# A decoder stack on one core: first layer with another order of loads, splits, norm sum and group products

## Chip, core and metric

The kernel runs on one core of one Trainium2 chip. The metric is the device time of one execution in microseconds (us); lower is better. The core has five engines, each with an instruction queue of its own that runs in order: TensorE (PE, its weight load shown as PEld), VectorE (DVE), ScalarE (ACT), GpSimd (POOL) and SyncE (SP, which here only starts DMA transfers). They wait for one another by semaphores.

## What is computed

A stack of layers on x of 256 tokens by 1024 features, all in float32. The change touches the first layer only:

```python
def diff_pool_layer(x, ...):
    proj = rms_norm(x, norm_g) @ w_in                 # 1024 -> 2048: q, k, v, u of 512 each
    q, k = rms_norm(q per head, q_g), rms_norm(k per head, k_g)
    lam = exp(sum(lp[0]*lp[1])) - exp(sum(lp[2]*lp[3])) + lam_init
    a_out = diff_attention(q, k, v, lam, lam_init, sub_g)   # 4 heads, softmax 0 minus lam * softmax 1
    b_out = pool_mixer(u, w_group, pool_scale)        # 4 groups: window mean minus token, @ w_group, * scale
    return x + concat(a_out, b_out) @ w_out
```

Behind it come a gated FFN with a short convolution, a sliding-window attention layer, two more FFNs, a layer of convolution and forgetting attention, another FFN and a norm (seven phases in all: L0, F0, L1, F1, F2, MIX, F3).

## The kernel before

**Data.** The activations X lie features-first (8 tiles of 128 features by 256 tokens). All weights come in one stream of chunks of 128x2048 float32 (1 MB each): chunk i goes into raw buffer i mod 3, ACT copies it into a rounded high part `whi` (`high(i)`, line 971), DVE subtracts to get the low part `wlo` (`low(i)`, line 1473). The activations are split alike: `Ghi` on ACT is X times the norm's gain, `Glo` on DVE is the rest. Each product is three matmuls (`three`, line 300: high by high, high by low, low by high). SP sends chunk i once `low(i-3)` is done (line 288). The norm's factor is not needed by the matmuls: it multiplies their result, so the projection starts before the sum of squares is known.

**Start (`first`, lines 1086 and 1577).** SP sends X and chunk 0 in four pieces each, in turns, then the ones matrix, chunk 1 in halves, chunk 2, and three tables for later (bias_a, wgroup, invcnt). ACT sends the first gain (`par[:, 0:8]`), the rest of `par`, and the rest of `cst`. Then ACT makes, for each of the four pieces, two tiles of Ghi and then a quarter of whi; DVE follows with two tiles of Glo and a quarter of wlo. After chunk 1 the squares of X are made on ACT; POOL adds the first two, DVE adds the last two, POOL adds both sums (line 2165 on). DVE then makes the small gain products and the sum for lam (lines 1594 to 1606), ACT loads its table for Ln and Exp and takes the exponential.

**Projection (PE's `l0`, lines 598 to 632).** Output blocks of 256 columns, one chunk each; `half(b, i, h)` is one half of chunk i's eight k tiles for both 128-column blocks, 24 matmuls. Chunk 0 is done in two halves; within a half all four k tiles of the first block come before the second block. The ones matmul for the norm (`norm_sum`) stands between the two halves of chunk 1. After it ACT makes the factor (`norm_log`, line 992, which loads the table again) and DVE evacuates the first blocks (`take`). From there heads follow: squares, `blocks`, `q_factor` (ACT), `scale` (DVE), `score` (PE), `bias_in` (DVE), `exps` (ACT), `combine` (DVE), `turn` (PE transpose), `value` (PE).

**Order.** There is no planner: each engine's order is written out by hand (PE 598 to 655, ACT 1133 to 1178, DVE 1659 to 1697, POOL 2165 on). An instruction that waits holds everything behind it on its engine.

**End of the layer.** Four attention values (`value`, evacuated by ACT's `take`), four group products (`mix_groups`, split by `group` on ACT and DVE), four head norms (`norm_out`, `out`), and four chunks of the output projection (`rows`), each needing two tiles of Mhi and Mlo.

Of the kernel before, what the change touches and what calls it, by code (L numbers as in the profile page):

```python
# [5 lines left out]
ALU = mybir.AluOpType  # L6
# [4 lines left out]
P = 128  # L11
S = 256
# [11 lines left out]
for _n, _w in (("ab_norm", 8), ("c_norm", 8), ("f_norm0", 8), ("f_norm1", 8), ("ffn1_norm", 8), ("mix_norm", 8),  # L24
               ("ffn2_norm", 8), ("a_q", 1), ("a_k", 1), ("a_sub", 1), ("b_scale", 4), ("c_q", 1), ("c_k", 1),
               ("conv0", 3 * 44), ("conv1", 3 * 44), ("convb0", 44), ("convb1", 44), ("conv_w", 31 * 4),
               ("conv_b", 4), ("ln_g", 4), ("ln_b", 4), ("onc", 4), ("ona", 4), ("forget_b", 1), ("sinks", 32),
               ("lam", 256)):
    PAR[_n] = (_at, _w)
    _at += _w  # L30
# [95 lines left out]
def program(nc, x, wst, par_d, cst_d, bias_a_d, bias_c_d, invcnt_d, wgroup_d, fin_d, out):  # L126
    ctx = ExitStack()
    with ctx:
# [18 lines left out]
        X = sb("X", [P, DT, S])  # L147
# [68 lines left out]
        s_gain, s_par, s_cst, s_ones = sem("s_gain"), sem("s_par"), sem("s_cst"), sem("s_ones")  # L216
# [50 lines left out]
        def _(sp):  # L267
            for j in range(4):
                ws = slice(512 * j, 512 * j + 512)
                sp.dma_start(X[:, 2 * j:2 * j + 2, :], two(x[:, ws])).then_inc(s_xin[j], 16)  # L270
                sp.dma_start(raw[:, 0, ws], wst[0][:, ws]).then_inc(s_w0[j], 16)
# [5 lines left out]
            sp.dma_start(bias[:, 0:4 * S], bias_a_d).then_inc(s_ba, 16)  # L277
            sp.dma_start(wgroup, two(wgroup_d)).then_inc(s_wg, 16)
            sp.dma_start(invcnt, invcnt_d.rearrange("p (a b) -> p a b", a=4)).then_inc(s_ic, 16)
            for i in range(3, NCH):  # L280
# [8 lines left out]
                sp.dma_start(raw[:, i % NR, w], wst[i][:, w]).then_inc(s_raw[i % NR], 16)  # L289
            for n, (t, h) in enumerate(((0, 0), (0, 1), (1, 0), (1, 1))):  # L290
# [5 lines left out]
        def _(pe):  # L296
# [11 lines left out]
            def half(b, i, h, ph=None):  # L308
# [5 lines left out]
                for n in range(2):  # L314
                    for k in range(4 * h, 4 * h + 4):
                        if n == 0 and ph is not None:
                            pe.wait_ge(s_glo, 8 * ph + k + 1)
                        if n == 0 and i < 2 and k % 2 == 0:
                            pe.wait_ge(s_lo, k // 2 + 1 if i == 0 else 5 + k // 4)
# [3 lines left out]
                if h == 1:  # L323
                    last.then_inc(s_used, 1)

# [27 lines left out]
            def norm_sum(ph, by_log):  # L353
                pe.wait_ge(s_sum, SUMS[ph])
                if ph == L0:
                    pe.wait_ge(s_ones, 16)
                else:
                    pe.wait_ge(s_x, 4 * ph)
# [187 lines left out]
            def l0():  # L546
# [87 lines left out]
                value(1)  # L634
# [3 lines left out]
                turn(2)  # L638
                pe.wait_ge(s_vt, 2)
# [322 lines left out]
        def _(act):  # L962
# [29 lines left out]
            def norm_log(ph, n):  # L992
                table()
# [92 lines left out]
            def first():  # L1086
                act.dma_start(par[:, 0:8], par_d[:, 0:8]).then_inc(s_gain, 16)
                act.dma_start(par[:, 8:NPAR], par_d[:, 8:NPAR]).then_inc(s_par, 16)
                act.dma_start(cst[:, 128:NCST], cst_d[:, 128:NCST]).then_inc(s_cst, 16)
                act.wait_ge(s_gain, 16)  # L1090
                for j in range(4):
                    ws = slice(512 * j, 512 * j + 512)
                    act.wait_ge(s_xin[j], 16)
                    for n in (2 * j, 2 * j + 1):
                        act.activation(Ghi[:, n, :], X[:, n, :], ACT.Copy, scale=col("ab_norm", n)).then_inc(s_ghi, 1)
                    act.wait_ge(s_w0[j], 16)
                    copy(whi[:, 0, ws], raw[:, 0, ws]).then_inc(s_hi, 1)
                for j in range(2):
# [3 lines left out]
                for j, o in enumerate((sq[:, 0, :], sq[:, 1, :], QR[:, 0, :], QR[:, 1, :])):  # L1102
                    act.activation(two(o), X[:, 2 * j:2 * j + 2, :], ACT.Square).then_inc(s_sq, 1)
                act.wait_ge(s_par, 16)
                act.wait_ge(s_lsum, 1)
                table()
                act.activation(lamt[:, 2:4], lamt[:, 0:2], ACT.Exp).then_inc(s_lexp, 1)

            def l0():
# [23 lines left out]
                high(2)  # L1133
# [327 lines left out]
        def _(dve):  # L1461
# [115 lines left out]
            def first():  # L1577
                dve.memset(eps[:, :], EPS).then_inc(s_eps, 1)
                dve.wait_ge(s_gain, 16)
                for j in range(4):  # L1580
                    ws = slice(512 * j, 512 * j + 512)
                    dve.wait_ge(s_xin[j], 16)
                    for n in (2 * j, 2 * j + 1):
                        dve.wait_ge(s_ghi, n + 1)
                        STT(Glo[:, n, :], X[:, n, :], col("ab_norm", n), f(Ghi[:, n, :]), ALU.mult, ALU.subtract).then_inc(s_glo, 1)
                    dve.wait_ge(s_hi, j + 1)
                    TT(wlo[:, 0, ws], raw[:, 0, ws], f(whi[:, 0, ws]), ALU.subtract).then_inc(s_lo, 1)
                for j in range(2):
# [752 lines left out]
```

## Time and profile before

| | |
|---|---|
| runs | 1067.52, 1065.29, 1066.82 us; median 1066.82 us |
| profiled execution | 1067.42 us, span 1065.6 us |
| mean granted TensorE clock | 0.994 of full |
| PE busy | 1027.7 us, 96% of the span |
| DVE, ACT, POOL busy | 732.4, 609.0, 345.7 us |
| read from memory | 181.39 MB |

The profiled execution is one run; its span is 1.8 us shorter than its own time. "Busy" counts instructions from start to end, and matmuls overlap, so a busy PE is not PE at its peak. A wait is given in square brackets behind an instruction: how long its engine idled before it, and who released it. The first layer fills about the first 100 us of the span.

### The profile page before, as it was taken

What the parts mean: (1) busy time and instruction counts of PE and PEld (TensorE: products, weight loads), DVE (VectorE), ACT (ScalarE), POOL (GpSimd) and SP (SyncE); (2) the same over time, 40 slices, a digit from 0 to 9 for tenths busy, and PEclk for the clock granted to TensorE, in tenths of its full rate; (3) what the DMA queues carried; (4) which work ended last, traced back from release to release, by engine and by line L of the source; (5) the groups of instructions that cost most, each with busy time, mean ns of one, the idle gap of its engine ahead of it and who ended that gap; (6) DMA issues with size and microseconds to landing.
All of it is one profiled execution on the core that took longest, in us unless ns stands there. A gap on an engine that the chain in (4) does not pass through costs nothing.

```text
span 1065.6 us, 17048 instructions
## 1 busy us (share of the span) xinstructions
PE 1027.7 (96%) x7078; PEld 941.7 (88%) x7078; DVE 732.4 (69%) x992; ACT 609.0 (57%) x841; POOL 345.7 (32%) x189
## 2 busy tenths in 40 slices
PE   6999999999999899999999999999999799999997
PEld 5889999998888799999888888888899598888886
DVE  5876898775548779887647766653799778666543
ACT  6765656653356657565436655543667776555631
POOL 1061264540000024545202455510148413555300
PEclk9999999999999999999999999999999899999999
DMA  8544665446432255555554655555245136555451
GB/s 320 205 147 141 255 212 185 166 151 237 159 119 80 69 189 198 205 191 164 197 193 141 242 186 181 198 197 193 102 160 167 72 120 219 190 183 197 139 177 40
DMA packets 27292, 183.53 MB, mean 172 GB/s; under 512 B 3152, under 2 KB 3280, under 8 KB 5968
## 3 DMA queue, kind: packets, MB, share of 16 engines
q1 hardware_dynamic: 26784, 181.74, 48.5%
q8 instruction: 56, 0.92, 0.3%
q10 hardware_dynamic: 432, 0.71, 0.2%
q14 instruction: 20, 0.16, 0.0%
HBM read 181.39 MB, written 1.05 MB: 171 GB/s over the span
## 4 chain that ended last, share of the span: by engine, by line
PE 85%; ACT 4%; DVE 4%; issue 3%; POOL 2%; DMA 1%; SPq 0%; DVEq 0%; POOLq 0%; ACTq 0%
PE psum L298 84%; POOL Y L2107 2%; ACT Pb L1075 1%; DVE Pb L1572 1%; DMA raw<-in_wst 1%; DVE wlo L1465 1%; ACT whi L969 1%; ACT Ob L1273 1%; DVE X L1471 1%; ACT Pb L1282 0%; DVE bias L1471 0%; DVE Pb L1468 0%; ACT PT L969 0%; PE psum L530 0%; POOL acc L2107 0%
## 5 line engine op out<-in xcount | busy, mean ns | idle before, releaser
L298 PE MATMUL psum<-G,whi 128*128 128x256 f32 (+1 forms) x2720 | 613.0, 313 | 9.7 <-DVE wlo L1465 9.7
L1465 DVE TENSOR_TENSOR wlo<-raw,whi 128x2048 fp32r<-128x2048 f32 (+1 forms) x172 | 389.3, 2275 | 205.0 <-ACT whi L969 204.9
L298 PEld LDWEIGHTS psum<-G,whi 128*128 128x128 f32 x2720 | 445.6, 190 | 44.2 <-DVE G L1471 8.4
L298 PE MATMUL psum<-G,wlo 128*128 128x256 f32 x1712 | 481.1, 281 | 0.0
L969 ACT ACTIVATE whi<-raw 128x2048 fp32r<-128x2048 f32 (+1 forms) x172 | 318.8, 1866 | 173.5 <-PE psum L298 164.4
L298 PEld LDWEIGHTS psum<-G,wlo 128*128 128x128 f32 x1712 | 324.1, 189 | 0.1
L298 PE MATMUL psum<-A,whi 128*128 128x512 f32 x528 | 183.2, 392 | 0.0
L2107 POOL TENSOR_TENSOR A<-Ab,A 128x512 fp32r<-128x512 f32 x44 | 124.9, 2839 | 139.6 <-ACT A L969 139.6
L2107 POOL TENSOR_TENSOR Ab<-Cb 128x512 f32<-128x512 f32 x44 | 117.5, 2670 | 116.1 <-ACT Cb L1010 116.1
L298 PE MATMUL psum<-A,wlo 128*128 128x256 f32 x528 | 147.3, 279 | 0.0
L298 PEld LDWEIGHTS psum<-A,whi 128*128 128x128 f32 x528 | 98.8, 187 | 22.0
L2107 POOL TENSOR_TENSOR acc<-sq 128x512 f32<-128x512 f32 x7 | 9.1, 1298 | 319.5 <-ACT sq L990 303.3
L298 PEld LDWEIGHTS psum<-A,wlo 128*128 128x128 f32 x528 | 99.6, 189 | 0.0
L1035 ACT ACTIVATE Cb<-Hb,par 128x256 f32<-128x256 f32 x88 | 47.4, 595 | 61.6 <-DVE Hb L1465 61.6
L1471 DVE SCALAR_TENSOR_TENSOR Cb<-Hb,par,Cb 128x256 f32<-128x256 f32 x176 | 78.0, 503 | 0.9
L298 PE MATMUL psum<-Mhi,whi 128*128 128x256 f32 x192 | 55.5, 289 | 1.0 <-DVE Mlo L1465 1.0
L298 PE MATMUL psum<-whi,A 128*128 128x512 f32 x176 | 54.6, 390 | 0.0
L298 PE MATMUL psum<-Mhi,wlo 128*128 128x256 f32 x192 | 54.3, 283 | 0.0
L298 PE MATMUL psum<-Mlo,whi 128*128 128x256 f32 x192 | 54.3, 283 | 0.0
L969 ACT ACTIVATE Cb<-psum 128x512 f32<-128x512 f32 x44 | 25.7, 589 | 48.5 <-PE psum L298 48.5
L2107 POOL TENSOR_TENSOR Y<-Y,Ob 128x256 f32<-128x256 f32 x41 | 41.6, 1015 | 12.2 <-ACT Ob L1273 4.7
L1465 DVE TENSOR_TENSOR Cb<-psum,Cb 128x512 f32<-128x512 f32 x44 | 29.8, 684 | 22.9 <-ACT Cb L969 22.9
(176 smaller groups left out, 1005.5 us busy)
## 6 DMA issues: line engine op xcount, KB each, us to landing
raw<-in_wst SPq DMA_DIRECT2D x165, 1024.0 KB, 4.9
bias<-in_bias_c SPq DMA_DIRECT2D x1, 2048.0 KB, 8.7
raw<-in_wst SPq DMA_DIRECT2D x3, 512.0 KB, 7.5
X<-in_x SPq DMA_DIRECT2D x4, 256.0 KB, 6.6
raw<-in_wst SPq DMA_DIRECT2D x4, 256.0 KB, 6.9
out<-bias SPq DMA_DIRECT2D x4, 256.0 KB, 2.0
bias<-in_bias_a SPq DMA_DIRECT2D x1, 512.0 KB, 11.1
bias<-in_invcnt SPq DMA_DIRECT2D x1, 512.0 KB, 12.0
```

The source lines that it names most:

```text
L298: return pe.matmul(o, a, b, start=start, stop=stop, skip_group_check=True)
L969: return act.activation(o, i, ACT.Copy)
L1035: act.activation(Cb[:, p % 2, e, :], Hb[:, p % 2, e, 2:S + 2], ACT.Identity, scale=col(f"conv{conv}", 2 * 44 + ch), bias=col(f"convb{conv} ...
L1075: last = act.activation(Pb[:, e, m, c0:c1], Pb[:, e, m, c0:c1], ACT.Exp, bias=st[:, e, 4 + k_:5 + k_], accum_out=st[:, e, 8 + k_:9 + k_])
L1273: act.activation(PR[:, q % 4, :], UP[:, i, j:j + S], ACT.Copy, scale=col("conv_w", 4 * j + i)).then_inc(s_prod, 1)
L1465: return dve.tensor_tensor(o, a, b, op)
L1471: return dve.scalar_tensor_tensor(o, a, s, b, op0, op1)
L1572: dve.tensor_tensor_reduce(Pb[:, e, m, c0:c1], bank[banks[m]][:, c0:c1], bias_of(m)[:, S - nk:S], 1.0, init_of(m), ALU.add, ALU.max, st[:, ...
L2107: return pool.tensor_tensor(o, a, b, op)
```

## The change

The layout of the first layer is changed; what is computed stays the same.

- **Loads.** The first norm's gain moves out of `par` and stands in front of x in one array, so that it comes with the first piece of X. SP sends only the X pieces; chunk 0's four pieces are sent by ACT's queue, at the same time. `par` (now one transfer) goes behind chunk 3, bias_a behind chunk 4, wgroup and invcnt behind chunk 5. The rest of `cst` goes behind chunk 2.
- **Splits.** Per piece ACT makes one Ghi tile, the quarter of whi, the second Ghi tile; DVE likewise.
- **PE.** Chunk 0 is multiplied piece by piece (`first_chunk`): two k tiles for both column blocks, then the next piece. `norm_sum` stands behind chunk 1.
- **Norm sum.** First square ahead of chunk 1's split, the second between its halves. POOL adds squares 0, 1 and 2; DVE adds the fourth.
- **Table.** ACT loads Ln/Exp's table once, behind its four DMA starts; the two later loads are gone.
- **Small products.** The gains and lam's sum go into DVE's `l0` behind `low(2)`, lam's end behind `take(1)`. One `q_factor` moves ahead of `high(4)`, one `scale` ahead of `low(4)`.
- **End of the layer.** Groups stand between values: `mix_groups(0)` and `turn(2)` before `value(1)`, `mix_groups(3)` behind the first `rows`, `group` likewise on ACT.

```diff
+        gain_x = sb("gain_x", [P, DT + DT * S])
+        X = gain_x[:, DT:].rearrange("p (a b) -> p a b", a=DT)
@@ block.sync
             for j in range(4):
-                ws = slice(512 * j, 512 * j + 512)
-                sp.dma_start(X[:, 2 * j:2 * j + 2, :], two(x[:, ws])).then_inc(s_xin[j], 16)
-                sp.dma_start(raw[:, 0, ws], wst[0][:, ws]).then_inc(s_w0[j], 16)
+                ws = slice(512 * j + (DT if j else 0), 512 * j + DT + 512)
+                sp.dma_start(gain_x[:, ws], x[:, ws]).then_inc(s_xin[j], 16)
...
-            sp.dma_start(bias[:, 0:4 * S], bias_a_d).then_inc(s_ba, 16)
-            sp.dma_start(wgroup, two(wgroup_d)).then_inc(s_wg, 16)
-            sp.dma_start(invcnt, ...).then_inc(s_ic, 16)
+            sp.dma_start(cst[:, 128:NCST], cst_d[:, 128:NCST]).then_inc(s_cst, 16)
             for i in range(3, NCH):
...
+                if i == 3:
+                    sp.dma_start(par[:, :], par_d).then_inc(s_par, 16)
+                if i == 4:
+                    sp.dma_start(bias[:, 0:4 * S], bias_a_d).then_inc(s_ba, 16)
+                if i == 5:
+                    sp.dma_start(wgroup, ...); sp.dma_start(invcnt, ...)
@@ block.tensor
+            def first_chunk(b):
+                h3, l3 = weights(0, DT)
+                for j in range(4):
+                    for n in range(2):
+                        ws = slice(n * P, n * P + P)
+                        for k in (2 * j, 2 * j + 1):
+                            if n == 0:
+                                pe.wait_ge(s_glo, k + 1)
+                                pe.wait_ge(s_lo, j + 1)
+                            last = three(...)
...
-                half(5, 0, 0, L0)
-                half(5, 0, 1, L0)
+                first_chunk(5)
                 half(4, 1, 0)
+                half(4, 1, 1)
                 norm_sum(L0, True)
+                half(6, 2, 0)
                 pe.wait_ge(s_cst, 16)
-                half(4, 1, 1)
-                half(6, 2, 0)
                 blocks(0, 7)
...
                 value(0)
-                value(1)
                 pe.wait_ge(s_wg, 16)
                 pe.wait_ge(s_vt, 1)
                 mix_groups(0, 5)
                 turn(2)
+                value(1)
...
                 pe.wait_ge(s_m0, L0_M[4])
                 mix_groups(1, 5)
-                pe.wait_ge(s_m0, L0_M[6])
-                mix_groups(3, 4)
                 value(3)
                 norm_out(1)
                 rows(0, 2)
+                pe.wait_ge(s_m0, L0_M[6])
+                mix_groups(3, 4)
@@ block.scalar, first
-                act.dma_start(par[:, 0:8], ...); act.dma_start(par[:, 8:NPAR], ...); act.dma_start(cst[:, 128:NCST], ...)
-                act.wait_ge(s_gain, 16)
+                for j in range(4):
+                    act.dma_start(raw[:, 0, ws], wst[0][:, ws]).then_inc(s_w0[j], 16)
+                table()
                 for j in range(4):
                     act.wait_ge(s_xin[j], 16)
-                    for n in (2 * j, 2 * j + 1):
-                        act.activation(Ghi[:, n, :], X[:, n, :], ACT.Copy, scale=col("ab_norm", n))
+                    act.activation(Ghi[:, 2 * j, :], X[:, 2 * j, :], ACT.Copy, scale=gain_x[:, 2 * j:2 * j + 1])
                     act.wait_ge(s_w0[j], 16)
                     copy(whi[:, 0, ws], raw[:, 0, ws]).then_inc(s_hi, 1)
+                    act.activation(Ghi[:, 2 * j + 1, :], ...)
+                square(0, sq[:, 0, :])
                 for j in range(2):
                     copy(whi[:, 1, ws], raw[:, 1, ws]).then_inc(s_hi, 1)
+                    if j == 0:
+                        square(1, sq[:, 1, :])
-                (four squares, wait for par and lsum, table(), Exp for lam)
+                square(2, QR[:, 0, :]); square(3, QR[:, 1, :]); high(2)
@@ block.scalar, l0
                 norm_log(L0, 0)                       # without its table()
                 q_square(0)
                 q_square(1)
+                act.wait_ge(s_lsum, 1)
+                act.activation(lamt[:, 2:4], lamt[:, 0:2], ACT.Exp).then_inc(s_lexp, 1)
                 high(3)
+                q_factor(0, 7)
                 high(4)
-                q_factor(0, 7)
...
                 take(0)
+                group(0, 5)
+                turned(2)
                 take(1)
-                turned(2)
-                group(0, 5)
+                group(2, 4)
                 take(2)
-                group(2, 4)
                 turned(3)
                 out(0)
+                group(1, 5)
                 take(3)
-                group(1, 5)
@@ block.vector, first
-                TT(QR[:, 0, :], QR[:, 0, :], QR[:, 1, :], ALU.add).then_inc(s_sqa, 1)
-                (gains, lam's sum, lam)
+                dve.wait_ge(s_sum, 2)
+                TT(acc[:, :], acc[:, :], QR[:, 1, :], ALU.add).then_inc(s_sqa, 1)
@@ block.vector, l0
                 low(2)
+                gains()
                 take(0)
                 take(1)
+                lam()
                 low(3)
+                scale(0)
                 low(4)
-                scale(0)
@@ block.gpsimd, l0
-                pool.wait_ge(s_sqa, 1)
+                pool.wait_ge(s_sq, 3)
```

## Rows read from the trace of the kernel before

**Rows 1.** Page, part 4: chain that ended last, by engine
```profile
PE 85%; ACT 4%; DVE 4%; issue 3%; POOL 2%; DMA 1%; SPq 0%; DVEq 0%; POOLq 0%; ACTq 0%
```

**Rows 2.** Timeline of the start: start us, us, engine, line, what [idle before <-releaser]
```profile
4.55 0.47 SPq L271 DMA_DIRECT2D raw<-in_wst  x1
4.81 1.28 ACT L1095 ACT_TABLE_LOAD   x1 [4.81 <-DMA X<-in_x]
...
7.56 0.69 DVE L1465 TENSOR_TENSOR wlo<-raw,whi 128x512 fp32r<-128x512 f32 x1
...
8.40 0.77 PE L298 MATMUL psum<-G,whi 128*128 128x256 f32 x2 [8.40 <-DVE wlo L1465]
...
10.46 0.61 ACT L969 ACTIVATE whi<-raw 128x512 fp32r<-128x512 f32 x1
10.47 0.77 PE L298 MATMUL psum<-G,whi 128*128 128x256 f32 x2 [0.45 <-DVE wlo L1465]
...
11.81 0.62 ACT L969 ACTIVATE whi<-raw 128x512 fp32r<-128x512 f32 x1
...
20.04 1.13 PE L298 MATMUL psum<-acc,cst 128*128 128x256 f32 x4 [0.55 <-POOL acc L2107]
...
24.93 0.50 PE L298 MATMUL psum<-G,whi 128*128 128x256 f32 x2 [0.89 <-DVE wlo L1465]
```

**Rows 3.** DMA issues, one window each: out<-in, queue, count, KB, us to landing
```profile
raw<-in_wst SPq DMA_DIRECT2D x1, 256.0 KB, 7.1
par<-in_par ACTq DMA_DIRECT2D x1, 421.0 KB, 5.8
...
raw<-in_wst SPq DMA_DIRECT2D x1, 1024.0 KB, 9.4
```

**Rows 4.** Stretches: A:B us, length, (PE busy (x count),) PEclk, DMA share, GB/s
```profile
5.00:12.00 7.00, 1.00 1.04 393
...
8.40:12.30 3.90, 3.45 (x14) 1.00 1.05 402
13.00:19.00 6.00, 6.00 (x53) 1.00 1.03 414
```

**Rows 5.** Timeline of ACT and DVE around the norm's factor
```profile
22.57 1.28 ACT L966 ACT_TABLE_LOAD   x1
22.58 2.29 DVE L1465 TENSOR_TENSOR wlo<-raw,whi 128x2048 fp32r<-128x2048 f32 x1 [1.46 <-ACT whi L969]
...
24.89 1.29 DVE L1465 TENSOR_TENSOR QR<-psum,R 128x512 f32<-128x512 f32 x2
```

**Rows 6.** Timeline of DVE, PE and POOL, middle of the layer
```profile
45.45 0.68 DVE L1465 TENSOR_TENSOR QR<-psum,R 128x512 f32<-128x512 f32 x1
...
47.69 0.40 PE L298 MATMUL psum<-G,whi 128*128 128x256 f32 x2
...
53.21 2.61 POOL L2107 TENSOR_TENSOR T<-UP 128x271 f32<-128x271 f32 x1 [33.13 <-DVE UP L1465]
...
57.43 0.63 POOL L2107 TENSOR_TENSOR T<-UP 128x271 f32<-128x271 f32 x1
...
57.61 0.74 DVE L1471 SCALAR_TENSOR_TENSOR QK<-QR,gsc,sq 128x256 f32<-128x256 f32 x1 [0.35 <-ACT sq L1068]
...
59.37 0.18 DVE L1629 RECIPROCAL st<-st 128x4 f32<-128x4 f32 x1 [0.25 <-ACT Pb L1075]
...
62.76 2.83 DVE L1465 TENSOR_TENSOR wlo<-raw,whi 128x2048 fp32r<-128x2048 f32 x1
```

**Rows 7.** Timeline of the layer's end
```profile
68.77 0.84 ACT L1082 ACTIVATE Vt<-psum,rcol 128x256 f32<-128x256 f32 x2
...
70.31 0.91 PE L298 MATMUL psum<-PT,Vt 128*128 128x128 f32 x6 [0.90 <-ACT Y L1119]
...
75.14 0.70 PE L298 MATMUL psum<-UP,bias 128*128 128x256 f32 x2 [0.87 <-DVE Mlo L1471]
...
76.59 0.47 PE L298 MATMUL psum<-Mhi,whi 128*128 128x256 f32 x1
```

More of the change, by code:

```diff
@@ L23 @@
 _at = 0
[L24 removed]
+for _n, _w in (("c_norm", 8), ("f_norm0", 8), ("f_norm1", 8), ("ffn1_norm", 8), ("mix_norm", 8),
                ("ffn2_norm", 8), ("a_q", 1), ("a_k", 1), ("a_sub", 1), ("b_scale", 4), ("c_q", 1), ("c_k", 1),
@@ L289, in _ @@
                 sp.dma_start(raw[:, i % NR, w], wst[i][:, w]).then_inc(s_raw[i % NR], 16)
+                if i == 3:
[3 more added lines that the diff above has]
+                if i == 5:
+                    sp.dma_start(wgroup, two(wgroup_d)).then_inc(s_wg, 16)
+                    sp.dma_start(invcnt, invcnt_d.rearrange("p (a b) -> p a b", a=4)).then_inc(s_ic, 16)
             for n, (t, h) in enumerate(((0, 0), (0, 1), (1, 0), (1, 1))):
@@ L324, in half @@
                     last.then_inc(s_used, 1)
+            def first_chunk(b):
[7 more added lines that the diff above has]
+                                pe.wait_ge(s_lo, j + 1)
+                            last = three(bank[b][:, n * S:n * S + S], h3[:, k, ws], l3[:, k, ws], Ghi[:, k, :], Glo[:, k, :],
+                                         k == 0 and n == 0, k == DT - 1)
+                last.then_inc(s_used, 1)
             def wide(b, i, h, ph=None):
@@ L992, in norm_log @@
             def norm_log(ph, n):
-                table()
+                if ph != L0:
+                    table()
                 act.wait_ge(s_nrm, ph + 1)
@@ L1086, in first @@
             def first():
-                act.dma_start(par[:, 0:8], par_d[:, 0:8]).then_inc(s_gain, 16)
-                act.dma_start(par[:, 8:NPAR], par_d[:, 8:NPAR]).then_inc(s_par, 16)
-                act.dma_start(cst[:, 128:NCST], cst_d[:, 128:NCST]).then_inc(s_cst, 16)
-                act.wait_ge(s_gain, 16)
+                for j in range(4):
+                    ws = slice(512 * j, 512 * j + 512)
+                    act.dma_start(raw[:, 0, ws], wst[0][:, ws]).then_inc(s_w0[j], 16)
+                table()
                 for j in range(4):
@@ L1093, in first, with square @@
                     act.wait_ge(s_xin[j], 16)
-                    for n in (2 * j, 2 * j + 1):
-                        act.activation(Ghi[:, n, :], X[:, n, :], ACT.Copy, scale=col("ab_norm", n)).then_inc(s_ghi, 1)
+                    act.activation(Ghi[:, 2 * j, :], X[:, 2 * j, :], ACT.Copy, scale=gain_x[:, 2 * j:2 * j + 1]).then_inc(s_ghi, 1)
                     act.wait_ge(s_w0[j], 16)
                     copy(whi[:, 0, ws], raw[:, 0, ws]).then_inc(s_hi, 1)
+                    act.activation(Ghi[:, 2 * j + 1, :], X[:, 2 * j + 1, :], ACT.Copy, scale=gain_x[:, 2 * j + 1:2 * j + 2]).then_inc(s_ghi, 1)
+                def square(j, o):
+                    act.activation(two(o), X[:, 2 * j:2 * j + 2, :], ACT.Square).then_inc(s_sq, 1)
+                square(0, sq[:, 0, :])
                 for j in range(2):
@@ L1101, in first @@
                     copy(whi[:, 1, ws], raw[:, 1, ws]).then_inc(s_hi, 1)
[L1102 to L1107, printed above, removed]
+                    if j == 0:
+                        square(1, sq[:, 1, :])
+                square(2, QR[:, 0, :])
+                square(3, QR[:, 1, :])
+                high(2)
             def l0():
@@ L1641, in combine, with gains, lam @@
                     last.then_inc(s_prob, 1)
+                def gains():
+                    dve.wait_ge(s_par, 16)
+                    TS1(gsc[:, 0:1], col("a_q"), 0.125, ALU.mult)
+                    TS1(gsc[:, 1:2], col("c_q"), 0.125, ALU.mult)
+                    TS1(gsc[:, 2:3], col("a_sub"), 0.8, ALU.mult).then_inc(s_gsc, 1)
+                    l4 = par[:, PAR["lam"][0]:PAR["lam"][0] + 256].rearrange("p (a b c) -> p a b c", a=2, b=2)
+                    lt = T[:, 0, 0:128].rearrange("p (a c) -> p a c", a=2)
+                    TT(lt, l4[:, :, 0, :], l4[:, :, 1, :], ALU.mult).then_inc(*own.up())
+                    dve.wait_ge(s_vec, own.n)
+                    dve.tensor_reduce(lamt[:, 0:2], lt, mybir.AxisListType.X, ALU.add).then_inc(s_lsum, 1)
+                def lam():
+                    dve.wait_ge(s_lexp, 1)
+                    TT(lamt[:, 4:5], lamt[:, 2:3], lamt[:, 3:4], ALU.subtract).then_inc(*own.up())
+                    dve.wait_ge(s_vec, own.n)
+                    TS1(lamt[:, 6:7], lamt[:, 4:5], 0.8 - 0.6, ALU.add).then_inc(s_lam, 1)
                 def take_u(c):
@@ L2293, in cols @@
         return a.reshape(-1, P).T
-    put("ab_norm", cols(v["ab_norm"][0]))
     put("c_norm", cols(v["c_norm"][0]))
```

35 lines of the change are left out of this document (11 added, 24 removed).

## The prediction

> **What bounds the kernel now.** I read four views. The chain that ended last says that PE carries the time [rows 1]: a microsecond counts where PE stands still or starts late. So the timeline of the first layer comes next, for PE's waits. Up to the first output rows there are six: 8.40 us before the first matmul, 0.45 at 10.47, 0.55 at 20.04, 0.89 at 24.93 [rows 2], and two of about 0.9 at the layer's end, told below. Between 24.93 and those two it never waits. The third view, DMA issues with their landings, says what the early waits hang on. Chunk 0's last piece was sent at 4.55 and landed 7.1 us later, at 11.65 [rows 2, 3]; ACT took it at 11.81 [rows 2]. From 5 to 12 us the transfers run at 393 GB/s with the DMA engines' share at 1.04 [rows 4], so the first pieces are paced by bytes, not by starts. The fourth, the other engines' timeline, shows who releases PE later.
>
> **The start.** (1) The table load at 4.81 lasts 1.28 us and begins when X's first piece is there [rows 2]. In the changed kernel it runs right behind ACT's four DMA starts (about 0.45 us each, the length of SP's start [rows 2], so until 2.6) and ends near 3.9, before any data: hidden. Its cover is the 4.8 us of the first landing. (2) `par`, 421 KB [rows 3], and `cst` (530 columns of 128 rows by 4 bytes, 265 KB) no longer run among the first pieces. Of X and chunk 0, 2048 KB, the last then lands 686 KB earlier, at 393 GB/s 1.8 us: 11.65 becomes 9.9. A piece pair of 512 KB takes 1.3 us, so the pairs are in at about 5.5 to 6.0, 7.3, 8.6 and 9.9. That chunk 0 goes over the other queue saves starts, which were not the bound; I cost it at nothing. (3) X's first piece at 4.9; chunk 0's first I take at 5.5, since two 256 KB pieces now share the rate. Then whi 0.61, wlo 0.69 with hand-overs: PE starts at 7.0. Bounds: 6.4 if the weights land with X, 8.1 if they land at 6.6. The two Ghi tiles round the copy cost nothing: they fill the wait for the weights. Before it was 8.40: **-1.4**.
>
> **Chunks 0 and 1.** From 8.40 to 24.93 PE took 16.53 us. Its three waits sum to 1.89 [rows 2]; a matmul's record lasts 0.16 us beyond the start of the next, so by starts each wait is 0.16 longer: 2.4 in all. Without them 14.1. PE's slow beginning stays in: 14 matmuls in 3.45 busy us against 53 in 6.00 later [rows 4], a surcharge of some 1.8 us, though the granted clock stands at 1.00 in both stretches. I carry it over unchanged. ACT's pace is one piece per 1.35 us (10.46 to 11.81 [rows 2]), so pieces are ready on DVE at about 7.3, 9.3, 10.9 and 12.4. PE, four triples a piece, wants them from 7.0, 9.6, 11.5 and 13.0: no wait, chunk 0 ends at 14.4. For chunk 1 DVE is ready at 14.35, just in time. `norm_sum`, now behind both halves, waits for nothing if the sum is there by 20.2.
>
> **DVE against POOL.** POOL's first two sums now run while DVE splits chunk 1. The rows show that such pairs take turns: POOL's 0.63 us addition took 2.61 beside a split that had started just before, and a split of 2.29 took 2.83 when POOL was first [rows 5, 6]. By that, POOL's first sum waits until 14.35 and ends at 15.6, the second half of chunk 1 runs to 16.8, POOL's second sum to 18.1, DVE's own to 18.75, `low(2)` to 21.05. PE wants `low(2)` at 21.0. So `half(6,2,0)` starts at **21.1** where it was 24.93, **-3.8**. The Trainium skill ("SBUF — State Buffer", Who interferes with whom) has the rule: the pair of ports is an exclusive lock, and a DVE instruction with two SBUF inputs blocks a reading GpSimd one. The trace agrees by the 2.61. Without the rule `low(2)` would be there at 20.0 and PE at 21.0, so it takes 0.1 us and all the slack.
>
> **Norm factor and heads.** The second table load (1.28 at 22.57 [rows 5]) is gone from ahead of Ln; Ln and Exp follow the sum at 21.1, and `take(0)` starts at 22.05 instead of 24.89 [rows 5]: 2.85 earlier. The gains (six small DVE instructions, with hand-overs 0.9 us together; such a one lasts about 0.18 [rows 6]) fit between `low(2)` and this. lam's exponential costs ACT 0.2 us ahead of `high(3)`. So ACT and DVE run 2.6 us early, PE 3.8: PE gains 1.2 on them. Its closest claim on them in the middle is `take(3)`, which ended at 46.1 for matmuls at 47.7 [rows 6]: 1.5 us of slack, so it still does not wait. DVE loses its waits of 0.35 and 0.25 [rows 6], because PE is ahead: it reaches the last scores, and ACT the last exponentials, 3.25 early. `take_v(1)` starts at 65.5 where it was 68.77 [rows 7].
>
> **The order at the end.** `value(1)` needs `take(0)` and starts 1.5 us after `take_v(1)` as before. But `mix_groups(0)` and `turn(2)`, 0.5 and 0.3 us of PE by the length of the same instructions' neighbours (0.70 for two passes with their tail, 0.91 for six small matmuls [rows 7]), now lie under its wait of 0.90, and the 0.87 us wait at 75.14 [rows 7] falls away since `mix_groups(3)` comes behind 5.8 us of `rows`. I take 0.6 and 0.85: **-1.4**. Behind this the order is PE's own and its tiles come in time: tile 5 at 73.4 for 74.3, tile 1 at 79.1 for 81. Everything later moves as a block.
>
> **DMAs on SP's queue.** SP's waits for chunks 3 to 5 come earlier with the splits. The tables put behind them are wanted late: `cst` at 24.1 (lands near 16), bias_a at 33.4, invcnt at 50. Only `par` is close; it is a rival below.
>
> **Sum.** -3.25 (last exponentials) -1.4 = -4.65 us. The profiled execution took 1067.42, so 1062.8; it stands 0.6 above the median of 1066.82, from which the sum gives 1062.2. I say 1062.6.
>
> **Rivals.**
> (a) *Pieces land later.* If the two queues don't share evenly and X and chunk 1 run ahead of chunk 0, or w0's first piece needs until 6.6 and each wait reappears, PE gains 1.5 to 2.5 at the start instead of 3.8. With the end's 1.4 and what slack takes up: 1064 to 1065. For: the engines are full from 5 us. Against: fewer bytes in front. The Trainium skill ("DMA: Bandwidth & Descriptors", Issuing engines are not separate DMA queues) says that transfers of all queues interleave on the same 16 engines; the share of 1.04 agrees. That speaks for sharing, and against a gain from the second queue. Chance 0.13.
> (b) *The lock goes the other way.* If POOL's second sum gets its turn before the half split, or another operation is held too, `low(2)` comes at 22.3, PE waits 1.2, and the gains and `take(0)` come 1 us later: 1063.8. Chance 0.12.
> (c) *The table is loaded again* before the first copy, 1.28 us at X's landing as now: PE starts at 8.1 and the lost microsecond stays: 1063.8. Against: copies and squares behind the load at 22.57 ran without another. Chance 0.04.
> (d) *Slower: the gains hold DVE.* `gains()` waits for `par`, and behind it on DVE stand `take(0)` and all heads. `par` is now sent behind chunk 3, at about 12.1. By bytes: 3823 KB behind chunk 0's last piece, 10 us: 19.8, wanted at 21.1. Upper bound: chunk 3's 9.4 us [rows 3] and 1.1 for `par`'s bytes: 22.6, costing 1.5. Each later microsecond costs one; the gain is used up when `par` lands at 21.1 + 4.65 = 25.8, and at 28 the time is 1069. Nothing in the rows reaches that. With any mishap of that size, chance 0.04.
>
> **How the numbers follow.** Forecast 0.67, (a) 0.13, (b) 0.12, (c) 0.04, (d) 0.04. A measurement of this kernel tells about 0.2%, 2.1 us, from no change: faster is below 1064.7. The forecast, (b), (c) and half of (a) lie below, less a little for sizes that are off together: faster 0.85, same 0.11, slower 0.04. The range's lower end has PE start at 6.4, no lock, and DVE's waits in the middle shrinking too: 6 us off, 1060.9. The upper end takes in (b), (c) and most of (a): 1064.9.
>
> **What would show it.** PE's first matmul at 7.0; no wait of PE over 0.2 us until past 60; `low(2)` ending near 21; one table load in the layer's start, before 4 us; `take(0)` at 22; the wait before `value(1)` still there but short, none before `mix_groups(3)`; the first output rows at about 71.5. The prediction is wrong if ACT still waits for chunk 0's pieces, if DVE's first gain starts after 21.5, or if a new wait of PE stands ahead of `turn(3)`, where its probabilities come only just in time.

## The result, and the profile after

The changed kernel takes 1056.39 us (median of 4 runs, 1054.56 to 1058.33); the kernel before takes 1066.28 us beside it (4 runs). The ratio is 0.9905, with a 95% interval from 0.9893 to 0.9918: **faster by about 10 us**. The forecast was 1062.6, with 1060.9 to 1064.9 as its range. So the sign was right, but the time lies 4.5 us below the range, and more than half of the gain was not foreseen. The profiled spans are 1065.6 us before and 1056.5 after.

Part 4 of the page after, the chain that ended last, by engine:

```profile
PE 83%; DVE 7%; ACT 6%; issue 2%; POOL 1%; DMA 0%; DVEq 0%; ACTq 0%; POOLq 0%
```

PE still carries the time, as in [rows 1]. The timeline of the first layer after, with the columns of [rows 2]:

```profile
2.62 1.28 ACT L986 ACT_TABLE_LOAD   x1 [2.62 <-issue]
...
4.86 0.61 ACT L989 ACTIVATE whi<-raw 128x512 fp32r<-128x512 f32 x1
...
6.35 0.76 PE L304 MATMUL psum<-G,whi 128*128 128x256 f32 x2 [6.35 <-DVE wlo L1490]
...
13.34 1.81 POOL L2142 TENSOR_TENSOR acc<-sq 128x512 f32<-128x512 f32 x1 [12.90 <-ACT sq L1120]
14.24 1.99 DVE L1490 TENSOR_TENSOR wlo<-raw,whi 128x1024 fp32r<-128x1024 f32 x1 [0.24 <-ACT whi L989]
15.30 2.08 POOL L2142 TENSOR_TENSOR acc<-acc,QR 128x512 f32<-128x512 f32 x1
...
18.03 2.28 DVE L1490 TENSOR_TENSOR wlo<-raw,whi 128x2048 fp32r<-128x2048 f32 x1
...
19.77 1.02 PE L304 MATMUL psum<-acc,cst 128*128 128x256 f32 x4
20.23 0.27 DVE L1493 TENSOR_SCALAR gsc<-par 128x1 f32<-128x1 f32 x3
20.44 0.59 PE L304 MATMUL psum<-G,whi 128*128 128x256 f32 x2
21.92 1.29 DVE L1490 TENSOR_TENSOR QR<-psum,R 128x512 f32<-128x512 f32 x2 [0.91 <-ACT R L1018]
...
64.36 0.81 ACT L1103 ACTIVATE Vt<-psum,rcol 128x256 f32<-128x256 f32 x2
...
65.86 0.91 PE L304 MATMUL psum<-PT,Vt 128*128 128x128 f32 x6 [0.53 <-ACT Y L1143]
...
69.65 0.94 PE L304 MATMUL psum<-PT,Vt 128*128 128x128 f32 x6 [0.37 <-ACT PT L989]
70.67 0.47 PE L304 MATMUL psum<-Mhi,whi 128*128 128x256 f32 x1
```

What to see here: one table load, under the first transfers; PE's first matmul at 6.35, where it was 8.40 [rows 2]; `half(6,2,0)` at 20.44, where it was 24.93 with a wait of 0.89; `take(0)` at 21.92 for 24.89 [rows 5]; the first output rows at 70.67 for 76.59 [rows 7]. The landings of the three transfers in question, one row each (KB, us from issue to landing):

```profile
gain_x<-in_x SPq DMA_DIRECT2D x1, 260.0 KB, 3.7
raw<-in_wst ACTq DMA_DIRECT2D x1, 256.0 KB, 3.9
par<-in_par SPq DMA_DIRECT2D x1, 421.0 KB, 7.3
```

**Where the time went outside the layer.** PE executes the same list of matmuls outside the first layer, so the n-th matmul of one trace can be set against the n-th of the other. After minus before, in us from the span's start (worked out from the traces' records):

```
n-th matmul          80    440    680   1700   2100   5400   6000    7000
time before        21.5   68.8  101.1  223.7  290.5  776.1  863.8  1041.4
after - before    -3.58  -4.83  -5.49  -8.78  -7.77 -10.52  -8.90   -9.10
```

By the layer's output rows (n=680) the gain is 5.5 us. Another 3.3 comes in the first FFN's up projection (to n=1700), 1 is lost in its down projection, and the second FFN does the same again. The 256-column products of L1 and MIX give 0.4 and 1.0 more, so that the gain stands at 11.2 at n=5600; some 2 of it are lost between 790 and 840 us. In none of these FFN stretches does PE wait: the matmuls themselves follow one another faster or slower. The view of stretches shows it: 150 to 200 us lies in F0's up projection, 235 to 275 in its down projection, 600 to 650 in F2. The columns are PE's busy time, its count, the granted clock, the DMA share and GB/s. First the kernel before:

```profile
150.00:200.00 50.00, 50.00 (x419) 1.00 0.51 178
235.00:275.00 40.00, 40.00 (x233) 1.00 0.59 208
600.00:650.00 50.00, 50.00 (x290) 1.00 0.57 193
```

and after:

```profile
150.00:200.00 50.00, 50.00 (x431) 1.00 0.58 206
235.00:275.00 40.00, 40.00 (x228) 1.00 0.60 212
600.00:650.00 50.00, 50.00 (x291) 1.00 0.55 192
```

PE is busy for the whole stretch and at a clock of 1.00 in all six, but in the first it does 431 matmuls instead of 419, in the second 228 instead of 233. Taken from start to start, the mean step of F0's and F1's up projection is 120.0 ns before and 116.7 after; of their down projection (a matmul of 512 columns and one of 256 in turns; the mean of both, per matmul) 173.3 before and 176.7 after; of F2 (the same turns) 173.3 in both. Below, such a triple stands as "steps up / down / F2". These matmuls run in fp32r, the rounded float32 of `whi`, `wlo` and G, each behind a weight load of its own.

The loss around 800 us is the granted clock. In every trace it falls there for some microseconds to half of full speed, and for how long differs between executions of one kernel. The kernel before, the same again (e4), the changed kernel, and the same again (e3):

```profile
785.00:850.00 65.00, 56.53 (x421) 0.92 0.33 114
785.00:850.00 65.00, 56.56 (x421) 0.92 0.34 114
785.00:850.00 65.00, 57.23 (x396) 0.87 0.28 98
785.00:850.00 65.00, 57.59 (x415) 0.89 0.28 98
```

By the records, the clock stands at half in this stretch for 10.2, 10.2, 17.1 and 13.7 us. The two traces of the changed kernel agree within about 0.3 us up to n=5800; then the second is ahead, by 11.07 at n=7000 where the first has 9.10. So up to 2 us of the table's last columns belong to that one execution (1058.33 us, the slowest of its four) and not to the change.

### The profile page after: what moved, and what is told of

Same layout as the page of the kernel before. It is cut to its first block, busy times and chain, and to the rows that moved or that the text cites. A ratio compares the mean times of both kernels' runs of the same rounds, so it can differ in the third digit from the quotient of the medians.

```text
span 1056.5 us, 17049 instructions
## 1 busy us (share of the span) xinstructions
PE 1023.8 (97%) x7078; PEld 938.3 (89%) x7078; DVE 732.9 (69%) x992; ACT 605.4 (57%) x839; POOL 349.5 (33%) x189
## 4 chain that ended last, share of the span: by engine, by line
PE 83%; DVE 7%; ACT 6%; issue 2%; POOL 1%; DMA 0%; DVEq 0%; ACTq 0%; POOLq 0%
PE psum L304 83%; DVE wlo L1490 2%; ACT whi L989 1%; ACT Pb L1096 1%; DVE gain_x L1496 1%; DVE Pb L1597 1%; POOL Y L2142 1%; ACT Ob L1298 1%; DVE Pb L1493 0%; ACT Pb L1307 0%; DMA gain_x<-in_x 0%; DVE G L1496 0%; DVE bias L1496 0%; ACT PT L989 0%; DVE QK L1496 0%
## 5 line engine op out<-in xcount | busy, mean ns | idle before, releaser
L304 PE MATMUL psum<-G,whi 128*128 128x256 f32 (+1 forms) x2720 | 603.9, 310 | 6.4 <-DVE wlo L1490 6.3
L304 PE MATMUL psum<-A,whi 128*128 128x512 f32 x528 | 185.5, 396 | 0.0
L2142 POOL TENSOR_TENSOR A<-Ab,A 128x512 fp32r<-128x512 f32 x44 | 130.8, 2973 | 135.4 <-ACT A L989 135.4
L2142 POOL TENSOR_TENSOR Ab<-Cb 128x512 f32<-128x512 f32 x44 | 114.1, 2592 | 110.9 <-ACT Cb L1031 110.9
L2142 POOL TENSOR_TENSOR Y<-Y,Ob 128x256 f32<-128x256 f32 x41 | 41.6, 1015 | 13.7 <-ACT Ob L1298 6.1
```

The source lines that it names most:

```text
L304: return pe.matmul(o, a, b, start=start, stop=stop, skip_group_check=True)
L2142: return pool.tensor_tensor(o, a, b, op)
```

## The experiments

The diff has one side effect that the first runs follow up. `gain_x` holds 8 floats in front of X, so X and the two tiles behind it in SBUF (G2 for the high and low FFN activations, and `cst`, whose first 128 columns are the ones matrix of every norm sum) each lie 32 bytes further back in every partition; `par` is 32 bytes shorter, so that all behind it lies as before. Theory A: this shift sets the pace of the matmuls. Rival B: how the program starts, or its instruction stream, sets it. Rival C: it varies from run to run.

**e1: the shift alone, in the kernel before.**

```diff
+        gain = sb("gain", [P, DT])          # in front of X
...
-                act.dma_start(par[:, 0:8], par_d[:, 0:8]).then_inc(s_gain, 16)
+                act.dma_start(gain[:, :], par_d[:, 0:8]).then_inc(s_gain, 16)
```

> The kernel before, with one edit: the first norm's gain has a tile of its own (32 bytes a partition) in front of X, so that X, G2 and cst lie 32 bytes further on, exactly where the changed kernel has them; every order and every transfer stays. The two traces differ in the start-to-start step of the matmuls of the first up projection (120.0 ns before, 116.7 ns after) and of the first down projection (173.3 and 176.7 ns). Theory A, the step hangs on where G2 lies: 116.7 ns here too, and the time falls by the 3.6 us that the trace shows behind the first layer, to about 1062.7, with the first layer as before (first output rows at 76.6 us). Rival B, the step hangs on how the program starts or on its instruction stream: 120.0 ns and 1066.3 us as before. Rival C, it changes from run to run: either of the two, also between the repeated runs.

Measured: 1061.85 us against 1067.12, ratio 0.9948 (0.9933 to 0.9963). Up to n=680 it runs as before (-0.09), at n=1700 it is 3.38 ahead, and at n=5600, before the clock falls, 6.08. Its three stretches:

```profile
150.00:200.00 50.00, 50.00 (x431) 1.00 0.53 181
235.00:275.00 40.00, 40.00 (x228) 1.00 0.59 211
600.00:650.00 50.00, 50.00 (x291) 1.00 0.54 188
```

The counts are those of the changed kernel. **The shift alone gives 5.3 us**; none of this depends on the first layer's order. The start and the order of all instructions are those of the kernel before, so rival B falls; e2 shows it from the other side.

**e2: the changed kernel without the shift** (the gain in a tile of its own behind `cst`, with one small transfer more behind X's first piece).

```diff
-        gain_x = sb("gain_x", [P, DT + DT * S])
-        X = gain_x[:, DT:].rearrange("p (a b) -> p a b", a=DT)
+        X = sb("X", [P, DT, S])
...
+        gain_x = sb("gain_x", [P, DT])
```

> The changed kernel with the reverse edit: the gain has a tile of its own behind cst, so that X, G2 and cst lie where the kernel before has them, and one small transfer more runs behind X's first piece. Theory A (place of G2): the matmul step of the first up projection goes back to 120.0 ns and the time rises by about 3.6 us to 1060; the first layer keeps its order and its output rows start within 0.5 us of the changed kernel's 70.7. Rival B (start or instruction stream): 116.7 ns and 1056.4 us, plus up to 0.4 for the extra transfer.

Measured: 1062.26, ratio 0.9954 (0.9938 to 0.9971), so 4.9 us gained, and the stretches count as before. The expectation had the step right and the time 2.3 us too low, because it took the shift's worth from the first trace as 3.6:

```profile
150.00:200.00 50.00, 50.00 (x420) 1.00 0.56 192
235.00:275.00 40.00, 40.00 (x233) 1.00 0.64 226
600.00:650.00 50.00, 50.00 (x290) 1.00 0.54 189
```

This is the kernel that the forecast costed, with its 4.65. The two halves, 5.3 and 4.9, make 10.2 of the 10.8 that the changed kernel gains against the same runs (e3).

**e3 and e4: both kernels again**, unchanged, measured beside e1 and e2.

> The changed kernel, unchanged, once more. Theories A and B: the same steps as in its first profile, 116.7 and 176.7 ns, and 1056.4 us within 0.2%. Rival C (from run to run): another step in this profile, and runs several microseconds apart.

> The kernel before, unchanged, once more, for a second profile of it. Theories A and B: steps of 120.0 and 173.3 ns as in its first profile and 1066.3 us within 0.2%. Rival C: other steps.

Measured: 1056.32 (ratio 0.9896, 0.9882 to 0.9911) and 1066.98 (0.9999, 0.9989 to 1.0008), each with the steps that it had. Rival C falls for the steps; for the granted clock around 800 us it holds, as shown above.

**e5 to e8: which tile's place matters?** e5 puts the 32 bytes between G2 and `cst`, e6 between X and G2; e7 moves X, G2 and `cst` by 64 (and by 32 some small tiles behind them); e8 moves A2, the FFN's hidden activations, by 32 and nothing else. The edit in each is e1's, or:

```diff
+            sb("ahead_of_A2", [P, 8], F32, reg)      # e8
```

> The kernel before with the gain's 32-byte tile between G2 and cst: X and G2 stay, only cst moves by 32 bytes. Theory A1 (it is G2, the moving operand of all projections, whose place sets the step): matmul step of the first up projection 120.0 ns, time 1067 us as before. Rival A2 (the tile's 32 bytes anywhere, or cst's place): 116.7 ns and about 1062.

> The kernel before with the gain's tile between X and G2: X stays, G2 and cst move by 32 bytes. Theory A1: 116.7 ns in the up projections, 176.7 ns in the first two down projections, time 1062 us as with X moved too. Rival A3 (X's place, which only ACT and DVE read): 120.0 ns and 1067 us.

> The kernel before with 64 bytes ahead of X instead of 32, so that G2 lies 64 bytes off its old place; A2 stays where it is (two small tiles are merged to make room). Is the fast step bound to an odd multiple of 32 bytes? Theory A1a (the rows of 64 bytes count): 120.0 ns and 1067 us again. Rival A1b (any place other than the old one, a multiple of 128 bytes, is good): 116.7 ns and about 1062.

> The kernel before with 32 bytes ahead of A2, the moving operand of the down projections; G2 stays. Theory A1 (the place of the moving operand sets the step of the products that read it): up projections stay at 120.0 ns, the first two down projections change from 173.3 ns. Rival A4 (the down step hangs on G2's place too, by the history of the stream): 173.3 ns and 1067 us. No sign is forecast for the time: by up to 3.3 ns in each of some 350 matmuls of two phases, 2 us either way.

| run | moved | us | ratio (95%) | steps up / down / F2, ns |
|---|---|---|---|---|
| before | nothing | 1067.25 | 1 | 120.0 / 173.3 / 173.3 |
| e5 | `cst` 32 | 1074.21 | 1.0070 (1.0053 to 1.0088) | 120.0 / 176.7 / 176.7 |
| e6 | G2, `cst` 32 | 1061.70 | 0.9950 (0.9936 to 0.9965) | 116.7 / 176.7 / 173.3 |
| e7 | G2, `cst` 64 | 1068.45 | 1.0019 (1.0009 to 1.0028) | 117.8 / 176.7 / 175.5 |
| e8 | A2 32 | 1068.15 | 1.0010 (1.0000 to 1.0020) | 120.0 / 173.3 / 173.3 |

e6 equals e1: X's place does not matter. e7 met neither of its theories (its 175.5 is 176.7 in F2's up and 173.3 in its down projection). e5 kept the up step that its theory A1 expected, but neither time came: `cst` alone makes the kernel 7 us slower, in stretches whose long run of matmuls never reads `cst`:

```profile
150.00:200.00 50.00, 50.00 (x419) 1.00 0.52 177
235.00:275.00 40.00, 40.00 (x228) 1.00 0.59 201
600.00:650.00 50.00, 50.00 (x285) 1.00 0.57 199
```

The up projection keeps its 419; the down projection falls to 228 and F2 from 290 to 285. In F3, too, the mean step of the up projection rises from 173.3 to 176.7. So there are at least two things, one that hangs on G2 and one on something in `cst`; and they act together, since with both moved (e6) F2 and F3 keep 173.3.

e8 seems to do nothing, but the three steps leave out F3's last product, which reads A2 in 512 columns. There the mean step is 226.7 ns in the kernel before and 233.3 in e8, 1.7 us in all. The kernel before, then e8:

```profile
1000.00:1055.00 55.00, 55.00 (x252) 1.00 0.29 101
1000.00:1055.00 55.00, 55.00 (x246) 1.00 0.28 96
```

So A2's place counts as well, in that product.

**e11: `cst` moved as in e5, but the ones matrix left in its old place.** Theory S1: what matters in `cst` is the norm sum's read of the ones.

```diff
+        ones = sb("ones", [P, 128])[:, :]
+        gain = sb("gain", [P, DT])
-        cst = sb("cst", [P, NCST])
+        cst = sb("cst", [P, NCST - 128])
```

> The kernel that was 7 us slower (only cst moved by 32 bytes) with one edit: the ones matrix, the part of cst that the norm sums read, goes back to its old place in a tile of its own; identity, block matrix and mask stay moved. Theory S1 (the norm sum's matmul, reading ones 32 bytes off, leaves the slow step behind in all that follows): 173.3 ns down, time back at 1067. Rival S2 (another reader of cst, or the place of something else): 176.7 ns and 1074.

Measured: 1066.94, ratio 1.0001 (0.9992 to 1.0010), steps as before:

```profile
150.00:200.00 50.00, 50.00 (x419) 1.00 0.50 177
235.00:275.00 40.00, 40.00 (x233) 1.00 0.59 210
600.00:650.00 50.00, 50.00 (x290) 1.00 0.56 194
```

The whole 7 us of e5 hangs on the ones matrix, which is read by a few matmuls before each FFN (and by some in L0, L1 and MIX) and by none within the stretches. A short read sets the pace of hundreds of later matmuls. By the records the pattern of single steps changes directly behind F0's norm sum: in e11 the up projection goes 117, 118, 121, 120, 124 ns over and over, in e5 it goes 120 each time. The mean is the same, so the up projection's time does not show it; 960 matmuls later the down projection has 173.3 in e11 and 176.7 in e5.

**e9 and e13: the changed kernel with `cst` (and all behind it) 128 and 512 bytes further**, to see whether the fast up projection can be had with the fast down projection. e9 does it with one unused tile of 24 floats; e13 with three small tiles that lay elsewhere, and 8 floats.

```diff
+        sb("ahead_of_cst", [P, 24])        # e9
```

> The changed kernel with 96 bytes ahead of cst and 32 behind par: G2 keeps the place that gave 116.7 ns in the up projections, while cst and everything behind it lie 128 bytes on from the places of the kernel before, a whole multiple of 64. So far every kernel with cst off by 32 or 64 bytes had 176.7 ns in the first two down projections, every one with cst in its old place 173.3. Theory S (the place of cst, which the norm sum reads just ahead of them, leaves the slow step behind): 116.7 ns up and 173.3 ns down, about 2.3 us less than the changed kernel, 1054. Rival R (the down step hangs on G2's place or on the gain's tile): 176.7 ns and 1056.4.

> The changed kernel with cst, and all behind it, 512 bytes on from the places of the kernel before (three small tiles fill the room), G2 where the changed kernel has it. With 128 bytes the down step was 175.6 ns instead of 176.7 and the up step 117.0 to 117.8. Theory S (the place of ones alone sets the down step, with a period of 512 bytes or less): 116.7 ns up, 173.3 ns down, some 2 us less than the changed kernel. Rival (the down step hangs on G2 and ones together, and G2's 32 bytes keep it slow): 175 to 177 ns and 1056 to 1058 us.

Measured: e9 1057.62, ratio 0.9918 (0.9899 to 0.9937), steps 116.7 to 117.8 / 175.6 / 174.1; e13 1055.57, ratio 0.9902 (0.9886 to 0.9919), steps 116.7 / 176.7 / 173.3. Neither is told apart from the changed kernel (0.9905). The simple form of the theory, in which the down projection hangs on the ones' place alone, fell.

**e14 to e16: does an additional matmul do it, with nothing moved?** In the kernel before, each FFN's norm sum gets one more matmul, into columns that nothing reads. In e14 its weights lie 32 bytes off the ones; e15 is the control with the ones themselves; e16 is e14 with the additional one first.

```diff
-                    mm(bank[at(ph, 3)][:, 0:S], ones, acc[:, 0:S], True, True).then_inc(s_nrm, 1)
+                    mm(bank[at(ph, 3)][:, 0:S], ones, acc[:, 0:S], True, True)
+                    mm(bank[at(ph, 3)][:, S:512], cst[:, 8:136], acc[:, 0:S], True, True).then_inc(s_nrm, 1)
```

> The kernel before, no tile moved, with one matmul more behind the norm sum of each of the four FFNs: the same acc, but as weights cst from column 8 on, 32 bytes off the ones matrix, into a part of the bank that nobody reads (so nothing of the result changes). Theory S (a weight read 32 bytes off leaves the slower step behind): 176.7 ns in the down projections of F0 and F1 and in F2, as in the kernel whose cst had moved, and 1067 + 7 + 4 x 0.45 = about 1075 us. Rival T (such a read costs its own time only): 173.3 ns and 1069.

> Control to the kernel before it: the same extra matmul, with the ones matrix itself, in its old place, as weights. Theory S and rival T alike: 173.3 ns and about 1069 us. If the step changes here too, it is not the 32 bytes but any further matmul that shifts it.

> The extra matmul 32 bytes off ahead of the norm sum's own, which then reads ones in its old place last. Theory S1 (the last read counts): 173.3 ns down, about 1069 us. Rival S2 (an off-place read is kept and not undone by one in place): 176.7 ns and about 1075.

Measured: 1074.47 (1.0080, 1.0065 to 1.0095), 1073.88 (1.0081, 1.0066 to 1.0096) and 1076.90 (1.0104, 1.0089 to 1.0119), all three with steps 120.0 / 176.7 / 176.7. The control's stretches:

```profile
150.00:200.00 50.00, 50.00 (x419) 1.00 0.51 181
235.00:275.00 40.00, 40.00 (x228) 1.00 0.57 197
600.00:650.00 50.00, 50.00 (x285) 1.00 0.57 200
```

They count as e5's, though no tile was moved, and the up projection has e5's pattern of 120 each time. The control itself is what taught something here: in F0, F1 and F2 the 32 bytes are not needed, either additional matmul does it. F3 is different: its up projection stays at 173.3 in e14 and e15 and goes to 176.7 in e16 (as in e5), which is worth 2.1 of the 2 to 3 us by which e16 is slower than they are. e14 and e16 have the same matmuls there and differ in the order of two.

The additional matmuls take 1.7 us of their own (0.43 each; the group of norm sums takes 7.4 us in place of 5.7), and the slower steps in F0, F1 and F2 add 5.6 in the traces. e14's trace, whose clock stands at half as long as that of the kernel before (10.2 us), ends 7.1 us later. The medians say 8.4 (e15) because the runs of the kernel before beside these had a median of 1065.47, where it was 1067 elsewhere; all seven of them had a mean granted clock of 0.996 or more.

So **the pace of a long run of matmuls depends on which matmuls ran before it**, and the places of their operands act through that or beside it. Which property is carried over was not found. One rival stands untested: an additional matmul also moves every later instruction of PE's stream by one. It can't explain e5 against e11, or e14 against e16 in F3, where the counts are the same.

**e10 and e12: the layer's end and its start apart.** e10 is the kernel before with the new order of the end alone; e12 is e2 with the old one, so the start alone.

```diff
                 value(0)
-                value(1)
                 ...
                 mix_groups(0, 5)
                 turn(2)
+                value(1)
```

> The kernel before with the new order of the layer's end alone (groups between values, the last group product behind the first output rows, on PE and ACT). By the prediction's term: 1.4 us less than before, 1065.6, the wait of 0.87 us ahead of mix_groups(3) gone and the output rows 1.9 us earlier in the trace, 0.45 of it only moved. Rival (the order pays only when PE runs ahead of ACT): no difference, because PE waits the same time for take(0) and turned(3).

> The changed kernel with G2 and cst in their old places and with the old order of the layer's end: loads, splits, norm sum, table and small products alone. With G2 and cst in place the whole change gave 4.9 us. By the prediction's terms 3.25 of it come from here: 1064.0. Rival (the start gives all and the end nothing): 1062.3.

Measured: e12 1063.51, ratio 0.9971 (0.9960 to 0.9982), so 3.5 us, for an expected 1064.0. e10 1066.33, ratio 0.9997 (0.9988 to 1.0006), for an expected 1065.6: not resolved by its times as they stand. Its trace has the rows earlier, though:

```profile
74.08 0.94 PE L298 MATMUL psum<-PT,Vt 128*128 128x128 f32 x6 [0.37 <-ACT PT L969]
...
75.10 0.47 PE L298 MATMUL psum<-Mhi,whi 128*128 128x256 f32 x1
```

75.10 for 76.59, and -1.06 us at n=680. The two waits of about 0.9 are gone and a new one of 0.37, on ACT's evacuation for `turn(3)`, stands in their place. e12 shows both old waits again:

```profile
66.72 0.91 PE L305 MATMUL psum<-PT,Vt 128*128 128x128 f32 x6 [0.90 <-ACT Y L1144]
...
71.56 0.70 PE L305 MATMUL psum<-UP,bias 128*128 128x256 f32 x2 [0.87 <-DVE Mlo L1497]
...
73.01 0.47 PE L305 MATMUL psum<-Mhi,whi 128*128 128x256 f32 x1
```

Between e2 and e12 the medians differ by 1.25 us and n=680 by 1.17 (-4.75 and -3.58). The end's order is worth 1.1 to 1.2 in the traces. The medians of all runs show 0.7 of it (1066.33 for 1067.02); among the runs with a mean granted clock of 0.994 or 0.993 alone, e10's eight have a median of 1066.57 and the eleven of the kernel before 1067.64, which is 1.1.

## Why the prediction was right in part

**The start: right, a little short.** Forecast 7.0, measured 6.35. The table load is hidden, as said (2.62 to 3.90). The step that was too careful is the landing of chunk 0's first piece: I took 5.5, and it came at about 4.6, together with X's (3.9 and 3.7 us from their issues). ACT's queue sent it while SP's sent X, so the second queue, which I costed at nothing, is the likely giver of these 0.6 us; it was not tried alone. In e2, with one small transfer more, PE starts at 6.70. What was measured lies at the lower bound of 6.4.

**Chunks 0 and 1: right.** PE has no wait between 6.35 and 65.86. `half(6,2,0)` stands at 20.44 for a forecast of 21.1: the 0.66 of the start, carried through.

**DVE against POOL: the mechanism right, rival (b) not seen.** POOL's two sums take 1.81 and 2.08 us, and the half split between them 1.99 where the first half took 1.23. In the kernel before, the first sum, which ran almost alone, took 1.29:

```profile
16.62 1.29 POOL L2107 TENSOR_TENSOR acc<-sq 128x512 f32<-128x512 f32 x1 [16.18 <-ACT sq L1103]
```

The ends lie as turns would have them: the first half split at 14.01 (12.78 and 1.23), POOL's first sum at 15.15, the second half split at 16.23, POOL's second sum at 17.38. The Trainium skill ("SBUF — State Buffer", Who interferes with whom) has this as an exclusive lock of the shared port pair; the trace agrees. This is the order that I laid out, with each end 0.3 to 0.7 us earlier than forecast, as PE's start was: `low(2)` ends at 20.3 for 21.05. It costs PE nothing.

**Norm factor and heads: right, 1.1 too little at their end.** `take(0)` at 21.92 for 22.05, `take_v(1)` at 64.36 for 65.5. `take_v(1)` is 4.41 earlier, as much as PE (4.49 at `half(6,2,0)`): between `take(0)`, 2.97 earlier, and there ACT and DVE catch up 1.4 us where I had allowed 0.4. Which waits gave it was not broken down.

**Rivals (a), (c) and (d)** did not occur: pieces on time, no second load, `par` in at 19.3 (its 7.3 us behind an issue at 12.0; I had 19.8) and the gains at 20.23, directly behind `low(2)`.

**The end: right, too large.** Forecast -1.4, measured -1.1 to -1.2. The 0.87 wait fell away as said; what I named in the last sentence as a possible fault, a new wait ahead of `turn(3)`, is there with 0.37, and in the changed kernel 0.53 of the wait before `value(1)` stays.

**The sum for the layer**: forecast -4.65; measured -4.75 at n=680 in e2 (and -4.9 in its time; in between, its profiled execution lost 1.4 while the clock stood at half near 372 us, and got 2.0 back near 830, where it did so for 3.4 us less), where PE starts at 6.70 and `take_v(1)` at 65.08; and -5.5 in the changed kernel (4.41 at `take_v(1)` and 1.1 for the end).

**The step that failed** is "Everything later moves as a block." The prediction has no term for what the new tile `gain_x` does to the places of the tiles behind it; it put this at nothing, without a reason. The shift was worth -5.3 us by itself (e1), all of it far behind the changed layer: about -3.3 in each up projection of F0 and F1, +1 in each of their down projections, and -0.7 and -1.0 in L1 and MIX. That is 6.1 up to n=5600; in e1's trace 0.8 of it is given back at the lower granted clock around 830 us. No row of the trace of before could have given this size; but no row excluded it either, and nothing in the range stood for it. The range's lower end of 1060.9 allowed 6 us, the measured gain was 10.

**What stays open.** Shown are: the place of G2 changes the up projection's step, the place of the ones matrix the down projection's, F2's and F3's, the place of A2 that of F3's last product, and one additional matmul in each norm sum does in F0, F1 and F2 what the moved ones matrix did. Not shown is the rule: e7's in-between steps, F3 in e14 to e16, and e9 and e13, where the step of the down projection is 175.6 and 176.7 with `cst` 128 and 512 bytes on, do not fit one period or one overlap. Whether the change makes the granted clock stand at half for longer around 800 us is open too: the two traces of the changed kernel have 17.1 and 13.7 us of it, but e13, with the same first layer, has 10.2 like the kernel before.

## What to carry to other kernels

Where PE is the bound and never waits, compare the step from one matmul's start to the next in stretches that the change does not touch, before giving a difference to the part that was edited; a tile put in front of others is an edit to all of them. To cost a new layout of loads, add it once with the tiles left where they were (as e2 does): that run tells the schedule's worth from the layout's. The order of the start could be forecast here from landings and waits to within a microsecond; where two queues sent the pieces side by side, the first pair landed together. Before a difference of 1 or 2 us is read from one trace, compare for how long the granted clock stood at half in both.

## What the hardware showed that was not expected

- The step of back-to-back matmuls of 256 columns in fp32r, at a granted clock of 1.00 and without any wait, is 120.0 ns in one kernel and 116.7 in another that differs by 32 bytes in its tiles' places (e1). The Trainium skill ("TensorE: Matmul & The Clock Gate", Back-to-back issue gap) has the columns over 2.4 GHz plus 2.5 ns for an isolated gap, by an estimate 109 ns here, and says that in a stream of weight loads and matmuls the spacing is set by both; for 256 columns it gives no measured spacing. Both measurements are above 109, and they decide.
- The same with the down projection, 173.3 or 176.7 ns, and with the ones matrix (e5, e11: 7 us). The Trainium skill ("SBUF — State Buffer", Who interferes with whom) gives PE read ports of its own, shared with no other engine, and that section has no word on an operand's place. These runs show that places count, without showing how.
- It is a lasting effect: one more matmul before each FFN, 1.7 us in all, made the kernel 7.1 us longer in a trace of equal clock (e14) and 8.4 in the medians (e15).
- The granted clock stood at half for 17.1 and for 13.7 us around 800 us in two executions of the same kernel, which moved their ends by 2 us against each other.
- ACT's table load took 1.28 us, hidden or not.
